# Fused decoder block on one Trainium2 core: where the expert loop gathers the next tokens and adds the last expert's result

## The reference

```python
logits = (hf @ w_router + b_router)
top_v, top_i = lax.top_k(logits, 4)            # 4 of 32 experts for each token
gate = jax.nn.softmax(top_v, axis=-1)
...
gu = xb @ w_gu[e] + b_gu[e]                    # (tokens, 1024) x (1024, 2048)
g_lin = jnp.minimum(gu[..., :D_FF], 7.0)
u_lin = jnp.clip(gu[..., D_FF:], -7.0, 7.0)
act = g_lin * jax.nn.sigmoid(1.702 * g_lin) * (u_lin + 1.0)
yb = act @ w_down[e] + b_down[e]               # (tokens, 1024) x (1024, 1024)
y = y.at[row_tok].add(yb * row_gate)
...
return rms_norm(h + y, g_final)
```

## Time and profile before

| | |
|---|---|
| median of the three timed runs | 1365.77 us |
| the profiled execution's own time | 1364.8 us |
| its span, first to last instruction | 1362.9 us |
| TensorE busy | 1262.1 us (93%) |
| VectorE / ScalarE / GpSimd busy | 308.2 / 190.2 / 119.5 us |
| mean granted TensorE clock | 0.977 |
| first gate-up product of expert 0 | 407.63 us |
| last `yb` copy of the loop | begins at 1348.82 us |
| bytes moved, mean rate | 452.16 MB, 332 GB/s |

### The profile page before, as it was taken

One profiled execution on the slowest core, in us unless ns is written; L12 is line 12 of the kernel. 1 busy time (PEld: TensorE's weight loads), 2 busy tenths in 40 slices (PEclk: granted clock), 3 DMA queues, 4 the chain that ended last, 5 costly groups with the idle time before them and its releaser, 6 DMA issues.

```text
span 1362.9 us, 14536 instructions
## 1 busy us (share of the span) xinstructions
PE 1262.1 (93%) x5739; PEld 587.3 (43%) x5739; DVE 308.2 (23%) x440; ACT 190.2 (14%) x264; POOL 119.5 (9%) x64
## 2 busy tenths in 40 slices
PE   5998989999889999999999999999999899999986
PEld 5996766466453333333333333333333233333332
DVE  3825353211241121112111111211111111111113
ACT  3554464001210000001000000100000000000000
POOL 5755540000000000000000000000000000000000
PEclk9899989999979999999999999999999999999999
DMA  6433424900478999999999999999999999999992
GB/s 224 155 125 123 155 93 135 355 31 0 192 301 343 422 421 421 421 421 420 421 421 422 420 421 421 420 421 422 420 421 422 421 419 422 421 421 421 421 420 93
DMA packets 79001, 452.16 MB, mean 332 GB/s; under 512 B 7093, under 2 KB 7257, under 8 KB 29737
## 3 DMA queue, kind: packets, MB, share of 16 engines
q1 hardware_dynamic: 78200, 448.87, 81.1%
q0 software_dynamic: 720, 2.20, 0.6%
HBM read 450.00 MB, written 1.05 MB: 331 GB/s over the span
## 4 chain that ended last, share of the span: by engine, by line
PE 48%; SPq 27%; DMA 17%; DVE 3%; issue 3%; ACT 1%; POOL 1%; DVEq 0%; POOLq 0%; ACTq 0%
SPq L379 19%; PE ps L522 11%; PE ps L823 11%; DMA ring<-in_w_gu 8%; DMA kv<-in_w_gu 8%; SPq L384 7%; PE ps L511 6%; PE ps L857 6%; PE ps L769 3%; PE ps L795 2%; PE ps L803 2%; PE ps L537 1%; PE ps L552 1%; POOL w_lo L341 1%; PE ps L607 1%
## 5 line engine op out<-in xcount | busy, mean ns | idle before, releaser
L823 PE MATMUL ps<-ring,nT 128*64 128x512 f32 x768 | 176.0, 598 | 18.9 <-DMA ring<-in_w_gu 18.4
L823 PE MATMUL ps<-ring,xs 128*64 128x512 f32 x768 | 172.9, 595 | 11.1 <-DMA ring<-in_w_gu 11.0
L857 PE MATMUL ps<-ring,xbuf 128*64 128x512 f32 x768 | 170.1, 595 | 0.0
L1082 ACT ACTIVATE xbuf<-xbuf 128x512 f32<-128x512 f32 x32 | 20.1, 629 | 799.4 <-DVE xbuf L1463 799.4
L1463 DVE TENSOR_SCALAR xbuf<-ps 128x512 f32<-128x512 f32 x32 | 22.1, 692 | 474.0 <-PE ps L823 474.0
L823 PEld LDWEIGHTS ps<-ring,nT 128*64 128x64 f32 x768 | 51.5, 136 | 141.2 <-issue 84.3
L341 POOL TENSOR_TENSOR w_lo<-ring,w_hi 128x2048 fp32r<-128x2048 f32 x22 | 103.8, 4724 | 83.5 <-ACT w_hi L903 83.4
L823 PEld LDWEIGHTS ps<-ring,xs 128*64 128x64 f32 x768 | 53.0, 137 | 128.2 <-issue 92.4
L857 PEld LDWEIGHTS ps<-ring,xbuf 128*64 128x64 f32 x768 | 53.0, 137 | 115.5 <-issue 115.5
L410 POOL TENSOR_SCALAR ss<-ss 128x2 f32<-128x2 f32 (+1 forms) x6 | 1.1, 190 | 1092.8 <-DVE ss L1113 1086.2
L1481 DVE COPY xbuf<-ps 128x512 f32<-128x512 f32 x32 | 22.1, 692 | 322.2 <-PE ps L857 322.2
(11 more groups left out here) (272 smaller groups left out, 1278.3 us busy)
## 6 DMA issues: line engine op xcount, KB each, us to landing
ring<-in_w_gu SPq DMA_DIRECT2D x192, 1024.0 KB, 26.8
ring<-in_w_down SPq DMA_DIRECT2D x96, 1024.0 KB, 26.8
ring<-in_w_in SPq DMA_DIRECT2D x24, 1024.0 KB, 5.2
small<-in_w_gu SPq DMA_DIRECT2D x16, 1024.0 KB, 26.2
xn<-in_w_gu SPq DMA_DIRECT2D x16, 1024.0 KB, 26.2
gates<-in_w_gu SPq DMA_DIRECT2D x16, 1024.0 KB, 26.8
kv<-in_w_gu SPq DMA_DIRECT2D x16, 1024.0 KB, 27.1
small<-in_w_down SPq DMA_DIRECT2D x8, 1024.0 KB, 26.2
```

The costliest lines, as they stand in the source:

```text
L823: i = mm(ps[64 * half:64 * half + 64, 4 + q, :], xg[:, k, (j % GE) * SLOTS:(j % GE + 1) * SLOTS], w[:, q * FF + half * 512:q * FF + half * ...
L857: i = mm(ps[64 * half:64 * half + 64, 6, :], actT[:, c, fh * 64:fh * 64 + 64], w[:, k % 2, half * 512:(half + 1) * 512], start=(k == 0), s ...
```

## The change

On TensorE, `gather` moves from behind the eighth gate-up chunk to behind the fourth (k = 3), with its wait for `hot_ready`, and `combine`, with its wait for `yb_ready`, to behind the sixth (k = 5). On VectorE, the copy of the gathered tokens moves from behind the activation chain to ahead of it, and with it the wait for `gathered`. Nothing is added or removed.

```diff
@@ TensorE, experts(it) @@
                         i.then_inc(chunk_used, 1)
-                    if j % GE == 0:
-                        pe.wait_ge(hot_ready, it * 2 + (j // GE + 2))
-                    gather(2 * (j % GE))
-                    pe.wait_ge(yb_ready, n + 1)
-                    combine()
+                        if k == 3:
+                            if j % GE == 0:
+                                pe.wait_ge(hot_ready, it * 2 + (j // GE + 2))
+                            gather(2 * (j % GE))
+                        if k == 5:
+                            pe.wait_ge(yb_ready, n + 1)
+                            combine()
                     for b in range(TB):
                         i = nc.tensor.transpose(ps[:, 6, b * P:(b + 1) * P],
@@ VectorE, experts(it) @@
+                    dve.wait_ge(gathered, it * 8 + (j + 5))
+                    take_gathered(xgT[1 - j // GE], 2 * (j % GE))
                     dve.wait_ge(chunk_used, it * STEP_CH + (FRONT_CH + j * EXP_CH + KD))
                     V.tensor_scalar(gl, ps[:, 4, :], LIM, None, ALU.min).then_inc(gl_ready, 1)
@@
                                     sg.rearrange("s (i q k) -> s i k q", i=2, k=2), ALU.mult).then_inc(act_ready, 1)
-                    dve.wait_ge(gathered, it * 8 + (j + 5))
-                    take_gathered(xgT[1 - j // GE], 2 * (j % GE))
                     if j % GE == GE - 1:
```

## The result

The changed kernel takes 1501.89 us in the median of four runs (1500.05 to 1503.31), against 1365.62 us before. The ratio is 1.0997, with a 95% interval of 1.0977 to 1.1016: 136 us slower. The forecast was 1479 (range 1405 to 1508).

What follows compares the result with a forecast made beforehand. TensorE, no longer the transfers, was to bound the expert loop: 1364.8 us, plus 30.0 for the longer packed experts, 83 for drops to half clock and 1.0 from profiled execution to median, gave 1479 us; range 1405 to 1508.

Steps and rivals of the forecast that it cites:

- What bounds the kernel: Expert loop: transfers set the end before, at 30.25 us an expert; after, TensorE bounds from first to last, at 30.10.
- the 29.16 us worked out: Expert loop: the time of an expert packed tight on TensorE above which TensorE, not the transfers, decides the end.
- The lost cover: TensorE behind gate-up: gather and combine no longer cover VectorE's chain; 2.72 us idle, packed expert 2.84 longer, +30.0 us in all.
- VectorE's copy and the earlier needs: VectorE: moving the 0.68 us copy ahead of the chain is worth nothing; earlier needs of gather and combine stay hidden.
- The clock: TensorE, each expert's wait and bias: a drop to half clock in nearly each of 32 experts, 2.6 us each, 83 us.
- The upper price: Expert loop: 3.4 us for each drop to half clock, from 6.7 us at half clock behind thin work; total 1505 us.
- the five: TensorE in the kernel before: five idle times of 1.8 to 2.5 us, two of them followed by half clock.
- No falls: Rival, expert loop: TensorE bounds and the clock never drops to half; 1396 us, chance 0.12.
- Seldom falls: Rival, expert loop: TensorE bounds, the clock drops in half of the experts at 1.7 us each; 1423 us, chance 0.20.
- Transfers bound: Rival, expert loop: transfers still set the end, gather and combine fill waits for weights; 1365 us, no change, chance 0.05.
- release of slots: Rival, expert loop: transfers starve while TensorE frees no slot, a gap 1.12 us shorter gives back 36 us; 1330, chance 0.03.
- The page's two rules: Trainium skill: idle time in each loop trip drops the clock each time; transposes do not bring the clock up.

Runs made afterwards that it cites:

- the early gather: The changed kernel with the combine put back behind the last gate-up product, so only the gather moves among the gate-up products: 1367.93 us, ratio 1.0016.
- the product: One thrown-away product of the gather's kind, 0.48 us, added to the early gather in its 0.7 us idle time: 1365.13 us, ratio 0.9996.
- the dense fill: The changed kernel with four thrown-away products of the gather's kind (128 rows) ahead of the wait for `act_ready`: 1418.91 us, ratio 1.0405.
- the 32-row fill: The changed kernel with four thrown-away products of the bias's kind (32 rows) ahead of the wait for `act_ready`: 1492.98 us, ratio 1.0939.

## Why the prediction was right, and which terms were off

- **What bounds the kernel.** Right. The transfers' full rate is gone and TensorE never waits for weights; the two versions in which a packed expert with its falls stays below or about at the 29.16 us worked out (the early gather with and without the product) take the time of before, and the two whose periods are mostly 30.4 to 30.6 lie 29 and 36 us above it.
- **The lost cover.** Right in mechanism, a little short in size. The wait was forecast as 2.72 us idle and measured as 2.63; but the transposes start 3.08 us after the last gate-up product instead of 2.99, and the gate-up stretch with gather and combine takes 17.97 us instead of 17.80: the two added switches cost 0.29 beyond 13.84 + 3.84, not 0.12. The transposes took 0.02 more as well. Without a fall the period is 30.33 (the dense fill) where 30.10 was forecast. Over 32 experts that is 7 us: 37 instead of 30.
- **VectorE's copy and the earlier needs.** Right: no wait of TensorE's for `hot_ready` or `yb_ready`, and the chain starts 0.12 us behind the last gate-up product as before. The text did not see that the copy's move is worth something: left in place it costs 30 us more.
- **The clock.** The forecast of a fall in nearly each expert was right. The term that was mis-sized is its price. I took the mean of 1.7 and 3.4 us, 2.6; 22 of the 31 periods have the long one. What is left of 137.1 us (1485.96 − 1348.82) above the 37 is 100 us, 3.1 us an expert, where 83 was forecast. Long and short go with the place of the fall. In the 22 periods of 33.73 the clock fell some 1.0 us or more before the first down product (at 464.6 in the expert shown, 3.4 us before it); in the six of 32.04 it fell 0.2 to 0.8 us before it, near the bias's end. In the sixth expert the bias runs from 599.41 to 601.34 and the clock falls at 601.15, as the rows below show. What prolongs the long ones is open.

```profile
601.20:604.50 3.30, 3.30 (x10) 1.00 (x10) 0.00 (x0) 0.00 (x0) 0.00 (x0) 0.50 0.78 323
604.70:609.00 4.30, 4.30 (x24) 1.41 (x22) 0.00 (x0) 0.00 (x0) 0.00 (x0) 1.00 0.56 227
```

- **What the clock term was read from.** The upper price, 3.4 us, came out as measured, but not by its row: of the 6.70 us at half clock from 374.1, TensorE was busy for 3.67 alone, so that stretch can't have cost more than 1.8. That it fits the expert loop, where TensorE is busy throughout, is luck. And the kernel before had more idle times than the five: behind 2.86 us (to 175.40) and 2.20 us (to 271.15) the clock stood at 0.50 from 176.2 and from 271.7, and behind 1.80 us (to 207.46) at 1.00. With them a fall followed four of eight such times, among them the longest.
- **The rivals.** No falls would have been 1396; the dense fill, which comes nearest to it, took 1419 with some falls left. Seldom falls (1423) went by the length of the idle time, and the 32-row fill shows that this alone does not decide: at 0.68 us idle the clock fell all the same, in each of the 28 plain periods. Transfers bound (1365) and release of slots (1330) are out by the transfers' rate, which is lower after.
- **The page's two rules.** The Trainium skill's account of a clock that falls in each trip of a loop ("TensorE: Matmul & The Clock Gate", HAM oscillation) is what happened: there was a fall in each of the 31 periods, behind 2.6 us of idle time. The upper price, 3.4 us for each fall, gave 1505, nearer than the mean. That does not bear out the page's rule on transposes (PE-mode transpose) from which I had drawn it: every long fall here has 32-row products or an idle stretch beside its transposes, and no run separates them.

## What to carry to other kernels

An instruction that looks misplaced behind a burst of matmuls may be the cover of another engine's chain: before moving it, add up what is left between the burst and the first instruction that needs the chain's result. A wait of 2.6 us in 30 cost twice, once as idle time and then as half clock in the products behind it, and the second cost was the larger (100 of 137 us). Where a wait can't be avoided, dense products in it, even useless ones, can pay: they took off 83 us here, as many products over 32 rows 9.

## What the hardware showed that was not expected

- The clock fell in more than half of the experts with TensorE idle for only 0.72 us, beside 0.5 us of transposes and 1.9 us of 32-row products; one dense product of 0.48 us in that place kept it at full speed from 443 to 860 us.
- At nearly equal idle time (0.68 and 0.82 us) 32-row products gave mostly periods of 33.67 us and dense ones 30.33.
- The periods take few values (32.04 and 33.73 in the changed kernel, 28.32 and 30.0 with the early gather): a fall costs 1.7 or 3.4 us there and nothing between. From the second expert on the falls begin 0.2, 0.6, 0.9, 1.3 and 1.7 us into the bias, and the last of these is the short one; so it comes at every fourth or fifth expert. Why their place moves so is not settled.
